# First norm from row sums beside the loads, other norms with a Newton step on the bank of sums

## The reference, cut to what matters

```python
for l in range(DEPTH):
    mod = c_act @ w_ada[l] + b_ada[l]
    sh1, sc1, g1, sh2, sc2, g2 = split(mod, 6)
    h = rms_norm(x, norm1_g[l]) * (1.0 + sc1) + sh1
    proj = h @ w_in[l]            # q, k, v, index heads, z, xbc, dt, gates
    ...                           # sparse attention and a state-space scan, whose
    y = rms_norm(y by 4 groups, ssm_norm_g[l])   # output has a norm of its own
    x = x + g1 * (mixed @ w_out[l])
    h = rms_norm(x, norm2_g[l]) * (1.0 + sc2) + sh2
    x = x + g2 * ((silu(gate) * val) @ w_down[l])
# block of type two: mixer and MLP, each behind a norm of x
# rms_norm(x, g) = x * rsqrt(mean(x * x) + 1e-6) * g
```

## Time and profile before

| | us |
|---|---|
| median of 3 runs | 1836.68 (1833.19 to 1836.99) |
| profiled execution | 1837.2 |
| its span | 1835.6 |
| PE busy | 1691.9 (92%) |
| POOL busy | 1255.8 (68%) |
| DVE busy | 872.4 (48%) |
| ACT busy | 861.5 (47%) |

### The profile page before, as it was taken

The page is one execution under the profiler, slowest core; times in us unless marked ns, Lnnn a source line. Parts: engine busy times, 40 slices in busy tenths (PEclk is TensorE's granted clock), DMA queues, the critical chain, the costliest instruction groups (busy, mean ns, idle before and its releaser), DMA issues.

```text
span 1835.6 us, 33961 instructions
## 1 busy us (share of the span) xinstructions
PE 1691.9 (92%) x13290; PEld 1639.6 (89%) x13290; DVE 872.4 (48%) x1774; ACT 861.5 (47%) x1411; POOL 1255.8 (68%) x948
## 2 busy tenths in 40 slices
PE   8999998989989999899998989979999986579999
PEld 8998997989889999899997989879999984479999
DVE  2457576466445643567665475434431354532200
ACT  2254444554346653464454554346654442335532
POOL 1467965656569999567965656658988790048886
PEclk8699999989889999999998989989999896589999
DMA  7245753446436667446753557446656650035664
GB/s 271 85 150 165 247 181 121 162 160 219 137 128 210 229 200 250 122 145 184 253 167 121 162 176 232 121 122 178 184 173 186 212 171 15 1 92 172 184 184 128
DMA packets 85518, 302.75 MB, mean 165 GB/s; under 512 B 9840, under 2 KB 12528, under 8 KB 85104
## 3 DMA queue, kind: packets, MB, share of 16 engines
q1 hardware_dynamic: 85360, 300.59, 51.2%
HBM read 299.50 MB, written 1.05 MB: 164 GB/s over the span
## 4 chain that ended last, share of the span: by engine, by line
PE 76%; DVE 10%; POOL 4%; issue 3%; ACT 3%; DVEq 2%; DMA 1%; SPq 0%; ACTq 0%; POOLq 0%
PE gemm_bank L1441 62%; POOL w_lo L390 4%; PE turn_bank L1548 2%; PE turn_bank L1518 1%; PE score_bank L1518 1%; ACT w_hi L408 1%; PE outp_bank L1536 1%; DVE rstd_row L766 1%; DVE conv L746 1%; PE outp_bank L1695 1%; DMA ada_w<-in_w_ada 1%; DVE idx_score L746 1%; PE score_bank L1441 1%; PE outp_bank L1583 1%; DVE probs L933 1%
## 5 line engine op out<-in xcount | busy, mean ns | idle before, releaser
L390 POOL TENSOR_TENSOR w_lo<-w_raw,w_hi 128x512 fp32r<-128x512 f32 x944 | 1255.6, 1358 | 568.3 <-ACT w_hi L408 566.3
L408 ACT ACTIVATE w_hi<-w_raw 128x1024 fp32r<-128x1024 f32 x472 | 492.6, 1046 | 700.5 <-PE gemm_bank L1441 673.2
L1441 PE MATMUL gemm_bank<-h_hi,w_hi 128*128 128x256 f32 x2112 | 613.6, 291 | 41.4 <-DVE h_lo L746 16.2
L1441 PE MATMUL gemm_bank<-h_lo,w_hi 128*128 128x256 f32 x2112 | 604.9, 286 | 0.0
L1441 PE MATMUL gemm_bank<-h_hi,w_lo 128*128 128x256 f32 x2112 | 604.6, 286 | 0.0
L1441 PEld LDWEIGHTS gemm_bank<-h_hi,w_hi 128*128 128x128 f32 x2112 | 412.9, 196 | 52.3 <-DVE h_lo L746 17.0
L1441 PEld LDWEIGHTS gemm_bank<-h_lo,w_hi 128*128 128x128 f32 x2112 | 413.2, 196 | 0.1
L1441 PEld LDWEIGHTS gemm_bank<-h_hi,w_lo 128*128 128x128 f32 x2112 | 412.7, 195 | 0.0
L746 DVE SCALAR_TENSOR_TENSOR conv<-gemm_bank,params_sb,conv 128x255 f32<-128x255 f32 (+1 forms) x320 | 139.5, 477 | 186.6 <-ACT conv L681 130.5
L1441 PE MATMUL gemm_bank<-w_hi,h_hi 128*128 128x256 f32 (+2 forms) x704 | 207.8, 295 | 18.4 <-DVE h_lo L746 8.0
L1441 PE MATMUL gemm_bank<-w_lo,h_hi 128*128 128x256 f32 (+2 forms) x704 | 202.7, 288 | 0.0
(11 more groups left out here) (284 smaller groups left out, 2268.9 us busy)
## 6 DMA issues: line engine op xcount, KB each, us to landing
w_raw<-in_stream SPq DMA_DIRECT2D x458, 512.0 KB, 3.7
ada_w<-in_w_ada SPq DMA_DIRECT2D x80, 512.0 KB, 4.8
ada_first<-in_w_ada SPq DMA_DIRECT2D x16, 512.0 KB, 10.6
w_raw<-in_stream SPq DMA_DIRECT2D x8, 256.0 KB, 2.7
alibi_sb<-in_alibi SPq DMA_DIRECT2D x1, 1920.0 KB, 7.3
rows_sb<-in_rows SPq DMA_DIRECT2D x1, 1536.0 KB, 10.6
residual<-in_x_t SPq DMA_DIRECT2D x1, 1024.0 KB, 7.4
out_x<-residual SPq DMA_DIRECT2D x4, 256.0 KB, 4.4
```

The source lines that it names most:

```text
L390: ins = nc.gpsimd.tensor_tensor(w_lo[:, s, e], w_raw[:, s, e], w_hi[:, s, e].bitcast(f32), ALU.subtract)
L408: A(w_hi[:, s, 0:n], w_raw[:, s, 0:n], ACT.Copy).then_inc(hi_ready, 1)
L1441: ins = M(o, a, b, start=first and i == 0, stop=last and i == len(passes) - 1, skip_group_check=True)
```

## The change

- **Start.** DVE sums the scale's rows as loads arrive (`first_rows(0, range(8))`) and half of those of the shift; PE adds each `ada_acc` over the partitions (`first_sum`, 8 matmuls), and for the shift's other four tiles PE adds columns (`shift_columns`, 32 matmuls). The tiles of `ada_first` are rows of the weight matrix now. The loads are in another order: constants ahead of x, `params2` behind the last tile. The rows of the first norm's mean, root and Newton step stand between them.
- **Norms.** `Sqrt` on ACT and `reciprocal` on DVE go; ACT applies `Abs_reciprocal_sqrt` to the mean, which stays in the bank of sums, and DVE makes one Newton step of three operations (`newton`; `rsqrt` for other norms). A small activation (`table`) makes ACT load its table ahead.
- **Squares.** Six of the eight square sums stand ahead of the last chunk of the stage before (`last_unit`, and for the down units), the last two behind it; ACT squares tiles 4 and 5 one chunk earlier. `ada_sum` for n = 1 and 3 stands ahead of the output units.
- **h tile by tile.** DVE alternates `scaled(kt + 2)` and `low(kt)`; PE's `from_norm` waits for each of the first four tiles and feeds two units from it.
- **Scan's norm.** The `rsqrt` after `decay(16)` is cut in two rows, one after `decay(16)` and one after `decay(17)`. The second call stays on both rows.

```diff
-            for i in range(2):
-                load_first(i)
-            sp.dma_start(XT[:], x_t.rearrange("(k p) t -> p k t", p=P)).then_inc(x_full, 16)
...
+            load_first(0)
+            sp.dma_start(XT[:], x_t.rearrange("(k p) t -> p k t", p=P)).then_inc(x_full, 16)
+            for i in range(1, 6):
+                load_first(i)
...
             def rsqrt(r, v, w):
-                V.reciprocal(r, r)
-                dve.drain()
-                V.tensor_tensor(w, r, r, ALU.mult)
+                stt(w, r, -0.5, r, ALU.mult, ALU.mult)
                 dve.drain()
                 V.tensor_tensor(w, w, v, ALU.mult)
                 dve.drain()
-                V.tensor_scalar(w, w, -0.5, 1.5, ALU.mult, ALU.add)
-                dve.drain()
-                ins = V.tensor_tensor(r, r, w, ALU.mult)
+                ins = stt(r, w, 1.5, r, ALU.add, ALU.mult)
...
+            def newton(l, i):
+                b, k = O.use(l, i)
+                m, r = O.bank[b][:, 0:SEQ], rs[:, 0, :]
+                stt(m, m, -0.5, r, ALU.mult, ALU.mult)
+                dve.drain()
+                V.tensor_tensor(m, m, r, ALU.mult)
+                dve.drain()
+                stt(r, m, 1.5, r, ALU.add, ALU.mult).then_inc(O.read[b], 1)
...
+                scaled(0)
+                scaled(1)
+                for kt in range(KT):
+                    if kt + 2 < KT:
+                        scaled(kt + 2)
+                    low(kt)
...
+            def first_norm():
+                first_rows(0, range(KT))
+                mean(0, O_N1, 1)
+                first_rows(1, range(2))
+                dve.wait_ge(x_root, 1)
+                newton(0, O_N1)
+                first_rows(1, range(2, ROWS_SHIFT))
...
                 for h in range(16, 32):
                     decay(h)
-                    if h == 16:
-                        dve.wait_ge(y_root, 4 * l + 2)
-                        rsqrt(rs[:, 0:2, :], work[:, 0:2, 0:SEQ], work[:, 2:4, 0:SEQ])
+                    if h < 18:
+                        gi = h - 16
+                        dve.wait_ge(y_root, 4 * l + gi + 1)
+                        rsqrt(rs[:, gi, :], work[:, gi, 0:SEQ], work[:, 2 + gi, 0:SEQ])
...
+            def shift_columns():
+                for k in range(ROWS_SHIFT, KT):
+                    pe.wait_ge(first_full[KT + k], 16)
+                    for j in range(KT):
+                        M(shift_ps[:, j:j + 1], ada_first[:, KT + k, j * P:(j + 1) * P], c_act[:, k:k + 1],
+                          start=k == ROWS_SHIFT and j == 0, stop=False, skip_group_check=True)
...
+            def last_unit(l, u, xh, xl, n, norm_l, which):
+                for p in range(n):
+                    if p == n - 1:
+                        square_sums(norm_l, which, range(KT - 2))
+                    part(l, u, p, feature_chunk, xh, xl, n)
+                square_sums(norm_l, which, range(KT - 2, KT))
...
+                for kt in range(KT // 2):
+                    pe.wait_ge(h_ready, n + kt + 1)
+                    for v in (u, u + 1):
+                        ins = products(tile_of(chunk_at(l, v, 0), gemm_of(l, v), HH, HL, kt, kt), kt == 0, False)
...
             pe.wait_ge(c_silu, 1)
-            for a in range(KT, 2 * KT):
-                ada_first_column(a)
-                if a == KT + 5:
-                    square_sum_x(0, 0)
-            for a in range(KT):
-                ada_first_column(a)
+            square_sums(0, 0, range(KT))
+            first_sum(0, mod_ps[:, KT:2 * KT], scale_summed)
+            shift_columns()
+            first_sum(1, shift_ps, shift_summed, more=True)
```

More of the change, by code:

```diff
@@ L428, in sum_root @@
                 b, k = O.use(l, i)
-                act.wait_ge(O.read[b], k + 1)
-                A(rs[:, 0, :], rs[:, 1, :], ACT.Sqrt).then_inc(x_root, 1)
+                act.wait_ge(x_mean, 2 * l + which + 1)
+                A(rs[:, 0, :], O.bank[b][:, 0:SEQ], ACT.Abs_reciprocal_sqrt).then_inc(x_root, 1)
             def h_high(l, which, bias):
@@ L451, in residual_units @@
                 square(1, (l, u0))
-                ahead(l, chunks[5:7])
+                ahead(l, chunks[5:6])
                 square(2, (l, u0))
+                ahead(l, chunks[6:7])
+                A(table[:], ones[:, 0:1], ACT.Abs_reciprocal_sqrt)
                 square(3, (l, u0))
@@ L459, in down_units @@
                     for p in range(chunks):
+                        if squared and j == 3 and p == 1:
+                            square(2, (l, u0))
+                            A(table[:], ones[:, 0:1], ACT.Abs_reciprocal_sqrt)
                         if squared and j == 3 and p == chunks - 1:
-                            square(2, (l, u0))
                             square(3, (l, u0))
@@ L716, in _ @@
             act.wait_ge(og_in, 1)
-            A(root[:, 2, 0:6], small[:, 0:6], ACT.Sqrt).then_inc(og_root, 1)
+            A(root[:, 2, 0:6], small[:, 0:6], ACT.Abs_reciprocal_sqrt).then_inc(og_root, 1)
             turn_o(l, T2_OT)
@@ L771, in rsqrt, with mean @@
                 dve.drain()
-                V.tensor_scalar(w, w, -0.5, 1.5, ALU.mult, ALU.add)
-                dve.drain()
-                ins = V.tensor_tensor(r, r, w, ALU.mult)
+                ins = stt(r, w, 1.5, r, ALU.add, ALU.mult)
                 dve.drain()
                 return ins
+            def mean(l, i, full):
+                m = O.bank[O.use(l, i)[0]][:, 0:SEQ]
+                dve.wait_ge(o_full, full)
+                V.tensor_scalar(m, m, 1.0 / D, EPS, ALU.mult, ALU.add).then_inc(x_mean, 1)
+            def newton(l, i):
[6 more added lines that the diff above has]
+                stt(r, m, 1.5, r, ALU.add, ALU.mult).then_inc(O.read[b], 1)
+                dve.drain()
             def norm(l, which, g_col, scale_col, shift):
@@ L793, in norm @@
[L793 to L808, removed]
+                mean(l, i, 6 * l + (6 if which else 1))
@@ new lines, in norm, with scaled, low @@
+                dve.wait_ge(x_root, n + 1)
+                newton(l, i)
+                def scaled(kt):
+                    stt(sq[:, kt, :], XT[:, kt, :], gain[:, kt:kt + 1], rs[:, 0, :], ALU.mult, ALU.mult).then_inc(h_scaled, 1)
+                def low(kt):
+                    dve.wait_ge(h_hi_ready, n * KT + kt + 1)
+                    if shift is None:
+                        V.tensor_tensor(HL[:, kt, :], sq[:, kt, :], HH[:, kt, :].bitcast(f32), ALU.subtract).then_inc(h_ready, 1)
+                    else:
+                        stt(HL[:, kt, :], sq[:, kt, :], shift[:, kt:kt + 1], HH[:, kt, :].bitcast(f32),
+                            ALU.add, ALU.subtract).then_inc(h_ready, 1)
@@ L1509, in arrived, with first_sum @@
                 pe.wait_ge(pair.read[b], k + 1)
[L1511 to L1519, removed]
+            def first_sum(v, out, signal, more=False):
+                pe.wait_ge(first_used, KT + ROWS_SHIFT if v else KT)
+                for j in range(KT):
+                    ins = M(out[:, j:j + 1], ada_acc[:, v, j * P:(j + 1) * P], ones[:, 0:1], start=not more, stop=True,
+                            skip_group_check=True)
+                ins.then_inc(signal, 1)
+            def shift_columns():
+                for k in range(ROWS_SHIFT, KT):
+                    pe.wait_ge(first_full[KT + k], 16)
+                    for j in range(KT):
+                        M(shift_ps[:, j:j + 1], ada_first[:, KT + k, j * P:(j + 1) * P], c_act[:, k:k + 1],
+                          start=k == ROWS_SHIFT and j == 0, stop=False, skip_group_check=True)
             def ada_sum(n, out):
@@ L1526, in ada_sum, with square_sums @@
                 ins.then_inc(ada_summed, 1)
-            def square_sum_x(l, which):
+            def square_sums(l, which, tiles):
                 i = (O_N2 if which else O_N1) if l < DEPTH else (O2_N2 if which else O2_N1)
[L1530 to L1533, removed]
+                b, k = O.use(l, i)
+                out = O.bank[b]
+                if tiles[0] == 0:
+                    take(O, l, i)
+                for kt in tiles:
                     if kt % 2 == 0:
```

139 lines of the change are left out of this document (96 added, 43 removed).

## The result

| | us |
|---|---|
| before, median of 4 runs beside the changed kernel | 1834.93 (1831.10 to 1836.99) |
| after, median of 4 runs | 1775.53 (1764.97 to 1781.81) |
| ratio | 0.9678, 95% interval 0.9648 to 0.9708 |
| profiled execution of after | 1764.97, span 1763.0 |
| predicted | 1780, range 1764 to 1797 |

The kernel is 3.2% faster, and the forecast of 1780 lies 4.5 us from the median. The experiments show that it came so near by luck: one term of the sum was nearly empty, and something that the prediction didn't have gave about as much.

What follows compares the result with a forecast made beforehand. PE, busy 92% of the span, was taken as the bound, with savings in its waits and cheaper work. Terms 24.1 + 9.4 + 9.2 + 12 + 1.5 = 56.2 us off the median of 1836.68 gave 1780 us, range 1764 to 1797.

Steps and rivals of the forecast that it cites:

- start: Ahead of the first product of weights: it begins at 43.6 instead of 67.69 us, 24.1 us less, 21 to 26.
- five norms: Norms of x, n = 1 to 5: shorter arithmetic and waits save 2.0 or 1.8 us each, 9.4 us in sum.
- scan, first call, two layers: Scan's first norm: one row of 3.6 us instead of 7.7 for both, 4.6 us a layer, 9.2 us in all.
- scan, second call, two layers: Scan's second norm: three operations on both rows, PE's wait nearly gone, 6 us a layer, 12 us in all.
- heads' norms of the last block: Last block: two of five operations go ahead of the second scaling of heads, 1.5 us on a DVE chain.
- DVE's eight `sq`: In the start: begin near 29 next to POOL, take 11.1 us, until 40.3, close to the main path but not last.
- T + 6.9: At a norm of x: first products come 6.9 us after T, the end of the last product, where n = 1 took 13.3.
- DVE is 4.2 to 6.7 us ahead. PE's wait of 5 is nearly gone: Scan norm's second call: three operations take 2.6 to 5.1 us, slow pace (2.6) goes too; counted as 6 us a layer.
- Rival B: Downstream, POOL or the ring falls behind and half of all savings but the start is given back: 1796; chance 0.14.
- Rival C: At the start, DVE's rows arrive late or columns run slower, so PE starts at 55: 1792; chance 0.09.
- Rival D: After each norm, PE fed tile by tile pauses and stays at half clock: slower than before, up to 1893; chance 0.02.

Runs made afterwards that it cites:

- e9: Changed kernel with the start as before (old load order, columns on PE, no rows on DVE for layer 0): 1791.90 us, ratio 0.9780.
- e10: Changed kernel with the five norms of x from n = 1 on as before, `ada_sum` ahead of the squares: 1776.09 us, ratio 0.9685.
- e11: Changed kernel with the heads' norms and both calls of the scan's norm as before: 1785.58 us, ratio 0.9744.
- e3: The changed kernel again, unaltered, on the chip of the placing controls: 1775.17 us, ratio 0.9688 to the kernel before.
- e8: Changed kernel with only the scan norm's second call as before (`Sqrt`, reciprocal, four operations): 1776.72 us, ratio 0.9689.
- e2: Kernel before plus an unused one-column buffer, which moves h and all behind it by 32 bytes: 1818.06 us, ratio 0.9911.
- e4: Changed kernel with `table` laid into a free column of `small`, so no buffer moves against the kernel before: 1789.44 us, ratio 0.9765.
- e6: Changed kernel with a 32-byte buffer ahead of `w_hi` and `table` in `small`, so w and h move together by 32: 1794.43 us, ratio 0.9783.
- e5: Changed kernel with `table` 16 columns wide, so h and all behind it move by 64 bytes: 1773.62 us, ratio 0.9675.
- e12: Changed kernel with `ada_sum` of n = 1 and 3 between the last product and the last two square sums: 1768.81 us, ratio 0.9652.
- e7: Changed kernel with `y_scale(8..15)` ahead of `y_low(0..7)` on DVE: 1772.93 us, ratio 0.9667.
- e1: The kernel before, unchanged, profiled again beside the placing controls: 1827.85 us in one run.

## Why the prediction was right, and where it wasn't

| term | predicted | measured |
|---|---|---|
| start | 24.1 | 17.9 (e9); 22.4 against the profile of before |
| five norms | 9.4 | 8.8 in the stages; in the time -0.5, 7.0 at most (e10) |
| scan, first call, two layers | 9.2 | 9.1 in the stages (e11: 12.3 and 12.3, e3: 8.1 and 7.4) |
| scan, second call, two layers | 12 | 1.7 in PE's waits (e8: 9.8, e3: 8.1) |
| heads' norms of the last block | 1.5 | not tried |
| placing of h | 0 | 10.5 (e2), 14.3 (e4), 20.8 (e6 against e5) |

The whole was right: 56.2 predicted, 59.4 measured. The measured terms, with the start against the profile of before, make 22.4 + 8.8 + 9.1 + 1.7 + 14.3 = 56.3 of it. That this comes near 59.4 proves little: the start is 17.9 in e9, the placing has three values from 10.5 to 20.8, and the norms don't show in the time. Three terms had their mechanism right. **Start:** DVE was the pace of the rows but for 0.9 us of waits for tiles, one-column matmuls ran at 0.43 us, and neither ACT nor DVE's `sq` was last; PE's wait of 1.39 us for a tile was missing. The mis-sized part is the time of before, which I took from one profile: 67.69, and 64.36 in another. DVE's eight `sq` took 5.28 us and not 11.1, since POOL was converting for 2.7 us of it only, and that was off the path. **Norms:** T + 6.9 against T + 7.1, Newton three times 0.43. (In the working, 11.5 - 9.6 is 1.9 and not 1.8, 0.3 us for the three norms.) I had `ada_sum` at its new place as an uncovered cost of 1.7 us for n = 1 and 3; attention's output stage is 24.4 us long with it (e3) and 22.7 without (e12, e10), exactly that. **First call:** 3.4 us for a row next to POOL where I took 3.6.

The Trainium skill (GPSIMD Engine Reference, Specifications) says that GpSimd contends with VectorE's instructions that have two SBUF inputs. The traces agree: at n = 1 POOL was at work (499.45 to 501.94 in the chain), and `newton` with its mean in PSUM took 0.43 three times, while at the scan the operations on two SBUF inputs took 1.39 and 1.33 for the same 256 columns, and the eight `y_scale` of e7 took 9.30 and not 3.25. One case is milder: the operation that reads the same tile twice (`work<-rstd_row` of the other row, at 280.93) took 0.56 beside POOL, where 0.43 is its time without.

**What failed** is the step "DVE is 4.2 to 6.7 us ahead. PE's wait of 5 is nearly gone". DVE was ahead, by 6.5 us. But `y_low` has a second input, `h_hi` from ACT, and ACT waits until PE is done with the buffer. In the trace of before these two ended 0.6 us apart. I had read the chain, which names the last releaser only, and took DVE's whole lead, cut only to 6 us by what lies behind it, for what PE would gain. The term of 12 us measured 1.7. Rival B told of savings given back downstream, but by POOL and the ring; that isn't what took this one.

**What was missing** is the placing. The prediction has no line on the new buffer but for the table load. Without it the changed kernel takes 1789.4 (e4), 43 us under before by its ratio of 0.9765, and 40 us by that of e6. That is what the planned edits are worth, 13 to 16 less than my sum. Some 10 of these are the second call. Rival C priced a start at 55, it was 45.3. Rival D didn't come: 3.1 to 5.9 us at half clock behind a norm, about as before.

## What to carry to other kernels

Ahead of pricing a faster operation, list all that its consumer waits for, and when each was ready in the trace; the chain shows the last one, and the gain ends at the last but one. Compare medians of different chips by their ratios to a common kernel. A buffer that is declared in the middle moves all behind it: where PE is the bound, compare the products' pace before and after, with the placing kept, before the gain is put down to the edits, and try a few placings on purpose. Before a vector operation is moved into an idle stretch, look at what GpSimd does there.

## What the runs showed of the hardware

Products of 256 columns at the granted 1.00 ran at three paces, and what parted the slowest from the others was the distance between buffers in SBUF: 0.1201 us in three kernels with the distances of before, wherever h stood (e1, e4, e6), 0.1168 or 0.1179 with h and all behind it moved by 32 or 64 bytes against w (e2, e3, e5 and the other runs with that placing). The diff shows nothing of it; the count of records in a stretch does.
